# A gated delta stage rewritten with 64x64 array tiles, and MLPs whose two products alternate unit by unit

## The reference

```python
def c_mixer(h, w_in, conv_w, a_log, dt_bias, head_gain, w_out):
    qkv, gate, b, a = _split(h @ w_in, C_SIZES)          # 3072, 1024, 8, 8 columns
    qkv = jax.nn.silu(short_conv(qkv, conv_w))           # 4 taps over time
    q, k, v = _split(qkv, (GDN_QK, GDN_QK, GDN_VW))      # 8 heads of 128
    q, k = l2norm(q), l2norm(k)
    beta = jax.nn.sigmoid(b)
    log_alpha = -jnp.exp(a_log) * jax.nn.softplus(a + dt_bias)
    o = gated_deltanet(q, k, v, beta, log_alpha)
    o = rmsnorm(o, head_gain) * jax.nn.silu(gate)
    return o.reshape(B, T, GDN_VW) @ w_out

def gated_deltanet(q, k, v, beta, log_alpha):            # per chunk of tokens and head
    g = jnp.cumsum(log_alpha)
    decay = jnp.where(incl, jnp.exp(g[:, None] - g[None, :]), 0.0)
    lower = jnp.where(strict, beta[:, None] * (k @ k.T) * decay, 0.0)
    rhs = jnp.concatenate([v * beta, k * (beta * jnp.exp(g))], axis=-1)
    u, w = triangular_solve(lower + eye, rhs)            # (I + lower)^-1 rhs
    attn = (q @ k.T) * decay
    v_new = u - w @ S
    o = (q * jnp.exp(g)) @ S + attn @ v_new
    S = S * jnp.exp(g_last) + (k * jnp.exp(g_last - g)).T @ v_new

def sq_relu_mlp(h, w1, w2):                              # 1024 -> 4096 -> 1024, twice in the block
    return jnp.square(jax.nn.relu(h @ w1)) @ w2
```

## Time and profile before

| | |
|---|---|
| median of 3 runs | 1356.88 us (1355.76 to 1361.72) |
| the profiled execution | 1355.71 us, its span 1353.9 us |
| TensorE busy | 1293.4 us, 96% |
| VectorE, ScalarE, GpSimd busy | 816.3, 711.0, 129.0 us |
| read from memory | 203.05 MB, 151 GB/s over the span |
| chain that ended last | TensorE 84%, VectorE 9%, ScalarE 4% |

### The profile page before, as it was taken

The page is one execution under the profiler, slowest core; times in us unless marked ns, Lnnn a source line. Parts: engine busy times, 40 slices in busy tenths (PEclk is TensorE's granted clock), DMA queues, the critical chain, the costliest instruction groups (busy, mean ns, idle before and its releaser), DMA issues.

```text
span 1353.9 us, 20948 instructions
## 1 busy us (share of the span) xinstructions
PE 1293.4 (96%) x8592; PEld 1176.1 (87%) x8592; DVE 816.3 (60%) x1180; ACT 711.0 (53%) x1133; POOL 129.0 (10%) x138
## 2 busy tenths in 40 slices
PE   6999999999999979999999999988999999999997
PEld 6988899998879868888998879967999898899886
DVE  5776578884557555645554448877555545555444
ACT  5767566654566445545554346553225544555433
POOL 5000011110000000000110000023530000011000
PEclk8999999999999999999999999999999999999999
DMA  9433465555445424534655554531011463455550
GB/s 330 154 117 106 141 191 183 187 188 188 169 141 191 154 96 150 187 102 147 187 185 189 186 186 153 166 119 62 1 32 58 160 203 125 139 180 182 194 201 39
DMA packets 138353, 205.45 MB, mean 152 GB/s; under 512 B 3730, under 2 KB 114706, under 8 KB 138258
## 3 DMA queue, kind: packets, MB, share of 16 engines
q1 hardware_dynamic: 138258, 204.11, 45.9%
HBM read 203.05 MB, written 1.05 MB: 151 GB/s over the span
## 4 chain that ended last, share of the span: by engine, by line
PE 84%; DVE 9%; ACT 4%; issue 2%; DMA 1%; SPq 0%; POOL 0%; DVEq 0%; ACTq 0%
PE ps L301 39%; PE ps L363 27%; PE ps L381 6%; DVE weights_lo L280 2%; PE ps L2034 2%; PE ps L2048 2%; PE ps L2045 1%; ACT weights_hi L277 1%; PE ps L2062 1%; PE ps L1703 1%; PE ps L1725 1%; PE ps L485 1%; DVE split_arena L516 1%; DMA weights<-in_w_in 1%; ACT normed L902 1%
## 5 line engine op out<-in xcount | busy, mean ns | idle before, releaser
L280 DVE TENSOR_TENSOR weights_lo<-weights,weights_hi 128x1024 fp32r<-128x1024 f32 x379 | 468.3, 1248 | 243.0 <-ACT weights_hi L277 241.1
L301 PE MATMUL ps<-split_arena,weights_hi 128*128 128x256 f32 x2928 | 537.9, 286 | 8.9 <-DVE split_arena L516 8.0
L277 ACT ACTIVATE weights_hi<-weights 128x1024 fp32r<-128x1024 f32 x379 | 396.8, 1057 | 260.2 <-PE ps L363 184.8
L301 PEld LDWEIGHTS ps<-split_arena,weights_hi 128*128 128x128 f32 x2928 | 460.2, 193 | 14.9 <-issue 9.8
L301 PE MATMUL ps<-split_arena,weights_lo 128*128 128x256 f32 x1464 | 415.9, 284 | 0.0
L363 PE MATMUL ps<-weights_hi,split_arena 128*128 128x512 f32 x1040 | 288.8, 394 | 3.5 <-ACTq L1875 1.6
L301 PEld LDWEIGHTS ps<-split_arena,weights_lo 128*128 128x128 f32 x1464 | 282.8, 193 | 0.0
L363 PEld LDWEIGHTS ps<-weights_hi,split_arena 128*128 128x128 f32 x1040 | 193.5, 188 | 47.5 <-issue 6.9
L363 PE MATMUL ps<-weights_lo,split_arena 128*128 128x512 f32 x520 | 161.1, 390 | 0.0
L363 PEld LDWEIGHTS ps<-weights_lo,split_arena 128*128 128x128 f32 x520 | 97.6, 188 | 20.7
L1883 POOL TENSOR_TENSOR normed<-normed 128x512 f32<-128x512 f32 x32 | 34.1, 1065 | 493.6 <-ACTq L1875 493.6
(11 more groups left out here) (345 smaller groups left out, 1440.9 us busy)
## 6 DMA issues: line engine op xcount, KB each, us to landing
weights<-in_mlp_w SPq DMA_DIRECT2D x64, 1024.0 KB, 5.3
weights<-in_w_up SPq DMA_DIRECT2D x22, 1024.0 KB, 5.1
weights<-in_c_w_in SPq DMA_DIRECT2D x16, 1024.0 KB, 5.4
weights<-in_w_in SPq DMA_DIRECT2D x14, 1024.0 KB, 6.4
weights<-in_ab_w_in SPq DMA_DIRECT2D x12, 1024.0 KB, 5.4
weights<-in_w_down SPq DMA_DIRECT2D x11, 1024.0 KB, 4.8
weights<-in_xa_wv SPq DMA_DIRECT2D x8, 1024.0 KB, 4.8
weights<-in_xa_wq SPq DMA_DIRECT2D x8, 1024.0 KB, 5.3
```

Source lines behind the costliest of these rows:

```text
L277: act.activation(h, r, ACT.Copy).then_inc(s_hi, 1)
L280: dve.tensor_tensor(l, r, h.bitcast(F32), ALU.subtract).then_inc(s_lo, 1)
L301: mm = pe.matmul(o, w[:, k, :], x[:, k, :], start=(k == 0 and i == 0), stop=(k == DC - 1 and i == 2))
```

## The change

1. `c_g` is taken first, then k, q and v. The sums of squares become 16 products with 8 output rows (`head_select`), placed behind units 4 to 9. The gate rows are computed after unit 9 (`ROWS_AFTER`).
2. The norms of q and k and beta are no longer multiplied in: their logarithms go into the exponents (`CRK`, `CRQ`). Eight `products` of four selecting and four data products remain, four of them moved between the levels of the inverse.
3. The inverse is taken of the 64x64 diagonal blocks by 5 levels behind the first (`blocks`). Products of partitions 0 to 63 and of 64 to 127 alternate, each into its own half of PSUM's partitions. The off-diagonal 64x64 block of each matrix comes from two more sets of 16 products at the end. GpSimd masks two half-partition pieces per group.
4. The output gate is multiplied by columns, its eight parts between `products` and levels; v and k are turned there too and scaled by ScalarE.
5. The head norm is taken in the transposed layout from four products with ones (`head_sums`), in place of 16 per-head reductions and a turn, and key pieces stand between.
6. In both MLPs unit u-3 of the second product follows unit u of the first (`MLP_LAG`), the first in PSUM banks 4 to 7, the second accumulating in banks 0 to 3.

The diff, cut to its core:

```diff
-            cols("c_qkv", "c_w_in", range(0, 3072, 256))
             plan.append(("c_g", "gates", "half", 256))
-            rows("c_gate", "c_w_in", DC, 3072)
+            cols("c_qkv", "c_w_in", [*range(1024, 2048, 256), *range(0, 1024, 256), *range(2048, 3072, 256)])
+            cols("c_gate", "c_w_in", range(3072, 4096, 256))
...
-        cols(f"m1{l}", f"mlp_w1{l}", range(0, D_FF_2, 256))
-        rows(f"m2{l}", f"mlp_w2{l}", FF2_TILES)
+        for u in range(FF2_TILES // 2 + MLP_LAG):
+            if u < FF2_TILES // 2:
+                cols(f"m1{l}", f"mlp_w1{l}", [256 * u])
+            if u >= MLP_LAG:
+                plan.append((f"m2{l}", f"mlp_w2{l}", "rows", (2 * (u - MLP_LAG), 2, 0, D)))
...
+            for u in range(NM1 + MLP_LAG):
+                if u < NM1:
+                    cols_unit(f"m1{l}", u, HT, A + u % 4, free, turned(turn, pe))
+                if MLP_LAG <= u < NM1 + MLP_LAG - 1:
+                    chunk_product(2 * (u - MLP_LAG))
+                    chunk_product(2 * (u - MLP_LAG) + 1)
+            last_products()
...
+                for f in range(2):
+                    h = 2 * (i % 4) + f
+                    mm = pe.matmul(PS[0:8, A + 1 + i // 4, 0:T], HSEL[:, h, :], SQL[:, i % 2, f * T:(f + 1) * T],
+                                   start=(h == 0), stop=(h == 7))
+                mm.then_inc(named("l2_ss"), 1)
...
+            cols_unit("c_g", 0, HT, G + 3, lambda u: pe.wait_ge(s_x, 4 * 6), turned(9, pe))
+            for u in range(NCU):
+                cols_unit("c_qkv", u, HT, G + u % 4, free)
+                for i in SQUARES_AFTER.get(u, ()):
+                    sum_squares(i)
...
+            def products(n):
+                hg, c = n // 2 % 2, n % 2
+                r, q0 = (CRK, 8) if n < 4 else (CRQ, 0)
+                if n == 0:
+                    pe.wait_ge(named("c_silu"), 8)
+                elif n == 1:
+                    pe.wait_ge(named("c_row"), 3)
+                elif n == 2:
+                    pe.wait_ge(named("c_conv"), NCU)
+                elif n == 3:
+                    pe.wait_ge(named("c_prep"), 1)
+                elif n == 4:
+                    pe.wait_ge(named("c_prep"), 4)
+                for j in range(4):
+                    mm = pe.matmul(PS[:, MB[n], j * P:(j + 1) * P], sel[:, 4 * hg + j, :], r[:, tok(c)], start=True,
+                                   stop=True)
+                mm.then_inc(named("c_p"), 1)
+                for j in range(4):
+                    mm = pe.matmul(PS[:, MB[n] + 1, j * P:(j + 1) * P], QKV[:, 8 + 4 * hg + j, tok(c)],
+                                   QKV[:, q0 + 4 * hg + j, tok(c)], start=True, stop=True)
+                mm.then_inc(named("c_p"), 1)
...
+            def blocks(bank, lhs, rhs, told, rows=(0, 1)):
+
+                for s in range(2):
+                    for m in range(8):
+                        for hg in range(2):
+                            b = hg ^ s
+                            if b not in rows:
+                                continue
+                            r = slice(64 * b, 64 * b + 64)
+                            mm = pe.matmul(PS[r, bank + hg, 64 * m:64 * m + 64], lhs(r, hg, m), rhs(r, hg, m),
+                                           start=True, stop=True)
+                            if m == 7 and (s == 1 or len(rows) == 1):
+                                mm.then_inc(named(told), 1)
+
+            products(0)
+            products(1)
+            products(2)
+            gate_part(0)
+            products(3)
+            gate_part(1)
+            gate_part(2)
+
+            pe.wait_ge(named("c_lt"), 2)
+            pe.wait_ge(named("c_prep"), 2)
+            blocks(6, lambda r, hg, m: LT[r, 0, hg, m, :], lambda r, hg, m: ident[r, r], "c_ym")
+            gate_part(3)
...
+            for lvl in range(1, LEVELS):
+                pe.wait_ge(named("c_x"), 2 * lvl)
+                pe.wait_ge(named("c_lt"), 2 * lvl + 2)
+                if lvl == 1:
+                    pe.wait_ge(named("c_prep"), 3)
+                blocks(2, lambda r, hg, m: LT[r, lvl % 2, hg, m, :], lambda r, hg, m: XI[r, hg, m, :], "c_ym")
+                if lvl < 5:
+                    products(3 + lvl)
+                    gate_part(3 + lvl)
+                    value_turn(lvl - 1)
+                    pe.wait_ge(named("c_prep"), 4 + lvl)
+                    if lvl % 2 == 0:
+                        pe.wait_ge(named("c_tq"), lvl // 2)
                 else:
-                    pe.wait_ge(named("c_prep"), gi - 1)
-                for i, r in ((0, 7), (1, 2)):
-                    for j in range(4):
-                        mm = pe.matmul(PS[:, pb + i, j * P:(j + 1) * P], sel[:, 4 * hg + j, :], CR[r][:, tok],
-                                       start=True, stop=True)
-                    mm.then_inc(named("c_p"), 1)
-                for i, q0 in ((2, 8), (3, 0)):
-                    for j in range(4):
-                        mm = pe.matmul(PS[:, pb + i, j * P:(j + 1) * P], QKV[:, 8 + 4 * hg + j, tok],
-                                       QKV[:, q0 + 4 * hg + j, tok], start=True, stop=True)
-                    mm.then_inc(named("c_p"), 1)
-
-            for gi in range(4):
-                pe.wait_ge(named("c_lt"), gi + 1)
-                if gi == 0:
-                    pe.wait_ge(named("c_prep"), 4)
-                if gi >= 2:
-                    pe.wait_ge(named("c_x"), gi - 1)
-                for j in range(4):
-                    mm = pe.transpose(PS[:, 6 + gi % 2, j * P:(j + 1) * P], LT[:, gi, j, :], ident[:, :])
-                mm.then_inc(named("c_l0"), 1)
-
-            NL = 4 * (LEVELS - 1)
-
-            def y(n):
-                gi = n % 4
-                pe.wait_ge(named("c_x"), n + 1)
-                pe.wait_ge(named("c_lt"), n + 5)
-                if n >= 2:
-                    pe.wait_ge(named("c_y"), n - 1)
-                for j in range(4):
-                    mm = pe.matmul(PS[:, gi % 2, j * P:(j + 1) * P], LT[:, gi, j, :], XI[:, gi, j, :], start=True,
-                                   stop=True)
+                    key_turn(0)
+                    key_turn(1)
+                pe.wait_ge(named("c_ya"), lvl)
+                pe.wait_ge(named("c_yb"), lvl)
+                if lvl == 1:
+                    pe.wait_ge(named("c_xt0"), 2)
+                else:
+                    pe.wait_ge(named("c_xt"), 2 * (lvl - 1))
+                xt = lambda r, hg, m: XT[r, hg, m, :]
+                y = lambda r, hg, m: YI[r, hg, m, :]
+                blocks(4, xt, y, "c_pm", (0, 1) if lvl < 5 else (0,))
+                blocks(6, y, xt, "c_qm")
...
+            for hg in range(2):
+                pe.wait_ge(named("c_x"), 2 * LEVELS - 1 + hg)
+                for m in range(8):
+                    mm = pe.matmul(PS[64:128, 2 + hg, 64 * m:64 * m + 64], ATC[0:64, hg, m, 64:128], XI[0:64, hg, m, :],
+                                   start=True, stop=True)
                 mm.then_inc(named("c_ym"), 1)
-
-            def pq(n):
-                gi = n % 4
-                pe.wait_ge(named("c_y"), n + 1)
-                if n >= 2:
-                    pe.wait_ge(named("c_x"), n + 3)
-                if n < NL - 4:
-                    for j in range(4):
-                        pe.matmul(PS[:, 2 + gi % 2, j * P:(j + 1) * P], XT[:, gi, j, :], YI[:, gi, j, :], start=True,
-                                  stop=True)
-                for j in range(4):
-                    mm = pe.matmul(PS[:, 4 + gi % 2, j * P:(j + 1) * P], YI[:, gi, j, :], XT[:, gi, j, :], start=True,
-                                   stop=True)
-                mm.then_inc(named("c_pq"), 1)
-
-            for n in range(NL + 1):
-                if n < NL:
-                    y(n)
-                if n >= 1:
-                    pq(n - 1)
-
-            def quad(bank, terms, told):
+            key_turn(2)
+            key_turn(3)
+            for hg in range(2):
+                pe.wait_ge(named(("c_ya", "c_yb")[hg]), LEVELS)
+                pe.wait_ge(named("c_xt"), 2 * LEVELS - 3 + hg)
+                for m in range(8):
+                    mm = pe.matmul(PS[0:64, 4 + hg, 64 * m:64 * m + 64], YI[64:128, hg, m, :],
+                                   XF[64:128, hg, m, 64:128], start=True, stop=True)
+                mm.then_inc(named("c_pm"), 1)
...
+            head_sums(0)
+            head_sums(1)
+            key_pe(1, 0, 4)
+            head_sums(2)
+            head_sums(3)
+            key_pe(1, 1, 5)
...
+            def gate_rows():
+                act.preload_act_table_set(EXP_LN)
+                act.wait_ge(named("c_row"), 1)
+                act_then(act.activation(GR[3], GR[2], ACT.Exp))
+                act.activation(GR[3], GR[3], ACT.Ln, bias=one_c[0:40, 0:1]).then_inc(named("c_log"), 1)
+                act.activation(NEA[:, :], gate_p[0:40, 3:4], ACT.Exp).then_inc(named("c_log"), 1)
...
+                    for b in range(2):
```

(68 more changed lines are left out.)

648 lines of the change are left out of this document (367 added, 281 removed).

## The result

| | before | after |
|---|---|---|
| median us | 1356.32 (1354.43 to 1361.72, 4 runs) | 1338.14 (1337.54 to 1339.03, 4 runs) |
| profiled execution, us | 1355.71 | 1337.54 |
| its span, us | 1353.9 | 1335.6 |
| first unit of the stage, us | 813.61 | 811.68 |
| out projection, us | 1037.24 | 1016.87 |

The account below looks back on a forecast made before the run. TensorE was taken to bound the kernel. The stage falls from 223.6 to 185.8 work plus 11.5 waits, 197.3 us; the 26.3 gain, less 1.2 (key copy), plus 2 (MLPs), is 27.1, so 1329 us, range 1313 to 1350.

Parts of the forecast that it names:

- TensorE's work of the stage: From the changed stage's first unit to the out projection, TensorE's own work without waits was summed to 185.8 us.
- A pair of small tiles: In the inverse, two alternating 64x64 tile instructions run beside each other, 60 ns together; 480 pairs take 28.8 us.
- The wait before products(1): TensorE waits about 5 us before the second selecting product, for VectorE's last convolution and gate rows.
- The wait before level 1: TensorE waits about 2 us before the inverse's level 1, ended by GpSimd's masks and first XT.
- The half clock: A granted clock of one half after the 5 us wait, partly hidden behind VectorE, costs 1.5 us.
- Late waits: TensorE waits 2 us for copies at the inverse's fifth level and 1 us for the recurrence's copies.
- The key copy: In the out projection's second half TensorE waits 2.4 us for VectorE's late key copy, 1.2 more than before.
- The MLPs: Alternating both products removes idle time at the second product's start, 1 us per MLP; bounds gain 2, loss 5.
- tiles don't overlap: Rival: the inverse's 1056 small instructions run in turn at 60 ns, 1358 us, or at 55.8 ns, 1353; chance 0.14.
- A full tile's price: Rival: each small instruction of the inverse with its load costs 111.6 ns, giving 1412 us; chance 0.06.
- The small tiles don't hold the clock: Rival: half clock through the inverse's small products, 35 us twice as long for half of them, 1347 us; chance 0.05.
- Waits instead of work: Rival: VectorE and GpSimd bound the inverse's start, stalls 25 us not 11.5, idle TensorE slows, 1343 us; chance 0.15.

## Why the prediction was right, and where it was off

Each number of before in this section is the prediction's own.

- **TensorE's work of the stage, 185.8.** Right. The stage took 205.2, of which 2.88 + 4.56 + 0.4 are waits (the 0.4 in the recurrence, ended by ScalarE) and about 11 the price of half clock, an estimate worked out below. That leaves 186.4.
- **A pair of small tiles at 60 ns.** Right: 60 to the next burst, with a change of tile shape in it. A group of eight products took 2.00 us (946.67 to 948.67), forecast 1.98; levels 11.24 us apart, forecast 11.
- **The wait before products(1), 5.** It was 2.88, ended by VectorE as forecast. The prediction's own terms give 20 - 15.8 = 4.2, not 5; in the trace VectorE needs about 18.9 us (880.09 to 898.97) and TensorE 16.1.
- **The wait before level 1, 2.** It was 4.56, and GpSimd was at its end as forecast. The prices on GpSimd were too low: a mask of half the partitions took 1.47 us over the twelve, not 1.27, the two before them 3.51, and one XT 2.14; from 915.75 to 929.0 GpSimd needed 13.3 us where 10 were forecast. That the two waits sum to 7.4 against 7 is luck: each missed by over 2 us, in opposite directions.
- **The half clock, 1.5.** This is the term that was mis-sized. Behind the first wait two products took 7.74 us (899.08 to 906.82), where at full clock three bursts of 1.08 and a last one of 0.91 take 4.2; about 20 gate matmuls followed at 0.21 instead of 0.12: 5.5 in all. Behind the second wait 64 small instructions took 3.61 instead of 2.02, a product 3.7 instead of 2.0, some gate matmuls 0.7 more: 4.0. At the stage's start the clock was also at half for a short stretch: 1.5. Sum 11. The prediction had one fall behind the one long wait, and VectorE hiding part of it. There were two falls, and TensorE set the pace behind both: with the waits filled, the two stretches are 5.45 and 4.06 us shorter, as much as is worked out here, so nothing had hidden them. Together the waits and the clock come to 18.8 against 11.5; that is 7.3 of the 7.9 us that the stage is over its forecast. The step that failed is this one term, a size and not the mechanism.
- **Late waits, 2 + 1.** Of them only 0.4 came.
- **The key copy, 2.4.** 2.82 us, ended by VectorE's copy as forecast.
- **The head norm at nothing.** Right: TensorE's key parts and sums run up to 1016.87 without a gap.
- **The MLPs, a gain of 2.** 0.82 in each, 1.6; nothing lost in the alternation.

The account closes: the stage gives -18.4, the key copy +1.6, the MLPs -1.6, a short half clock at 1102 us, which before didn't have behind the same wait of 2.52 us, about +1.5, and the part ahead of the stage, without its MLP, -1.1. That makes -18.0 of the 18.2 measured.

Of the rivals, *tiles don't overlap* described the kernel with the tiles in turn well: it forecast 1358 at 60 ns an instruction, and that kernel has 1363 at 53, with the half clock on top. Its other form, one matmul in 55.8 ns, doesn't hold here, and neither does the 62 ns for a MATMUL that the prediction quotes from the Trainium skill, "TensorE: Matmul & The Clock Gate" (Part 1), for a core with hardware decoding off: a matmul instruction with its own load takes 30 ns. *A full tile's price* fell with it. *The small tiles don't hold the clock* fell too: the levels from 941 us on have 1.00 at 236 instructions in 11 us. *Waits instead of work* was the rival that came partly true: its size, 25 us, would be 1343, and 18.8 were measured. The prediction ends its forecast case at 1338, but its own bound of 25 us for the stalls gives 1342; the measured 1338.14 lies between.

**Open.** What decides whether the clock falls behind a wait: 2.82 us in the out projection and 3.27 in the kernel before had no fall behind them, 2.01 and 2.47 had, and 0.79 in the kernel with the waits filled. Why it fell at about 905 us in two kernels without an idle time ahead of it, and not in a third with the same order. Why it fell behind the wait of 1.28 us at the stage's start in the new kernel, when before had the same wait and no fall, and neither had the kernel with the masks first. Whether the MLPs' 1.6 us reach the total.

## What to carry to other kernels

Give a wait of the pacing engine two prices, its length and what the granted clock may give away behind it. Here 7.4 us of waits cost 9.5 more through the clock, in stretches that show a busy share of 97 to 100%, while other waits as long cost nothing more; so read the clock column before the busy one. Independent work that already exists is the best filling: three changes of order in the queues gave 12 us. And where a tile of the array is small, the order of the loops decides its price; alternate between the halves instruction by instruction.

## What the hardware showed

- Small matmuls that alternate between two diagonal 64x64 tiles take 30 ns an instruction with its load, and 53 ns when eight in turn use the same tile. The difference was 25 us in this kernel.
- What a wait costs in clock doesn't follow its length. Around idle times of 2.88 and 4.56 us the granted clock was at 0.50 for some 13.6 and 10 us, and the repeat of the new kernel showed the same; behind one of 2.01 us for some 10, behind 2.14 and 2.47 us for 3.4. Behind 1.72 us (in one trace), 2.82 us (out projection) and 3.27 us (the kernel before) it stayed at 1.00.
- Useless work paid where it kept the clock: 66 added matmuls of 256 columns made the kernel 5.6 us faster, though 18 more on top of the three changes of order gave no gain that the medians show. The Trainium skill, "TensorE: Matmul & The Clock Gate" (Loop structure matters more than you think), counts a wait for a DMA between matmuls as what lets TensorE go cold, and a copy by VectorE as harmless when the next matmuls follow at once. The traces agree with the condition: here the waits were for VectorE and GpSimd, with no DMA in them, and as the matmuls didn't follow at once, the clock fell all the same.
